# A delta rule with two matrix inversions interleaved half a period apart, and four smaller edits around it

## What is computed

```python
decay = exp(where(incl, g[..., :, None] - g[..., None, :], -inf))
m = where(strict, einsum('bhncd,bhnsd->bhncs', k_beta, k) * decay, 0.0)
t_inv = triangular_solve(eye + m, eye, left_side=True, lower=True, unit_diagonal=True)
...
def step(state, inp):                       # over 16 chunks of 64 tokens
    v_new = u_i - w_i @ state
    o = (q_i * exp(g_i)) @ state + a_i @ v_new
    state = state * exp(g_last) + k_dec.T @ v_new
...
scores = where(|k_pos - q_pos| <= WINDOW, q @ k.T * HD ** -0.5, -inf)
mx = maximum(max(scores), sink);  p = exp(scores - mx)
out = (p / (sum(p) + exp(sink - mx))) @ v
```

## Time and profile before

| what | us |
|---|---|
| median of three runs | 2195.47 |
| the profiled execution | 2197.01 |
| its span, first to last instruction | 2195.2 |
| TensorE (PE) busy | 2104.6, 96% |
| VectorE (DVE) busy | 1120.2, 51% |
| ScalarE (ACT) busy | 725.2, 33% |
| GpSimd (POOL) busy | 353.0, 16% |
| mean granted TensorE clock | 0.980 of full |
| `delta_and_window`, 336 to 716 us of the span | 380 |
| `mix_and_hidden_layer`, about 1332 to 2195 us | 863 |

### The profile page before, as it was taken

How to read it: one execution, slowest core, us unless ns; L and a number is a source line. 1 busy time by engine, 2 the same in 40 slices (tenths; PEclk the granted TensorE clock), 3 DMA queues, 4 the chain that set the end, 5 groups by cost and what they waited for, 6 DMA issues and landing times. The chain is left out here.

```text
span 2195.2 us, 33712 instructions
## 1 busy us (share of the span) xinstructions
PE 2104.6 (96%) x14274; PEld 1637.5 (75%) x14290; DVE 1120.2 (51%) x1724; ACT 725.2 (33%) x1344; POOL 353.0 (16%) x291
## 2 busy tenths in 40 slices
PE   7999997899998899999998999999999999999998
PEld 6888885567676687887775667778888888878877
DVE  6773335766756666563533664464433443442443
ACT  4113313333344334132314773452212212221221
POOL 3000003321322543021210323430000000000000
PEclk9999997999989899999999999999999999999999
DMA  6112322000000847712123103211111111111112
GB/s 217 48 48 86 96 87 92 1 2 2 2 2 2 302 139 275 266 40 58 59 78 150 52 17 135 77 58 48 39 58 48 38 57 51 43 39 53 49 34 101
DMA packets 186890, 167.40 MB, mean 76 GB/s; under 512 B 13472, under 2 KB 163828, under 8 KB 186100
## 3 DMA queue, kind: packets, MB, share of 16 engines
q1 hardware_dynamic: 180974, 146.75, 21.1%
q0 software_dynamic: 4784, 17.83, 2.1%
q10 hardware_dynamic: 982, 0.65, 0.1%
HBM read 138.48 MB, written 26.74 MB: 75 GB/s over the span
## 5 line engine op out<-in xcount | busy, mean ns | idle before, releaser
L250 PE MATMUL mix_acc<-mix_hi,w_hi 128*128 128x512 f32 x1040 | 415.0, 399 | 0.0
L252 PE MATMUL mix_acc<-mix_hi,w_lo 128*128 128x512 f32 x1040 | 409.3, 394 | 0.0
L251 PE MATMUL mix_acc<-m_lo,w_hi 128*128 128x512 f32 x1040 | 408.8, 393 | 0.0
L230 ACT ACTIVATE w_hi<-w_stage 128x1024 fp32r<-128x1024 f32 x154 | 162.6, 1056 | 463.3 <-PE mix_acc L252 247.2
L3178 DVE SCALAR_TENSOR_TENSOR hidden<-mix_acc,hidden_conv,hidden 128x1023 f32<-128x1023 f32 x88 | 112.8, 1282 | 263.5 <-ACT hidden L3127 262.0
L238 DVE TENSOR_TENSOR w_lo<-w_stage,w_hi 128x1024 fp32r<-128x1024 f32 x154 | 192.9, 1252 | 106.3 <-ACT w_hi L230 106.3
L250 PEld LDWEIGHTS mix_acc<-mix_hi,w_hi 128*128 128x128 f32 x1040 | 195.3, 188 | 52.0 <-issue 8.2
L252 PEld LDWEIGHTS mix_acc<-mix_hi,w_lo 128*128 128x128 f32 x1040 | 195.3, 188 | 45.7
L251 PEld LDWEIGHTS mix_acc<-m_lo,w_hi 128*128 128x128 f32 x1040 | 195.5, 188 | 43.4
L250 PE MATMUL acc<-h_hi,w_hi 128*128 128x512 f32 x400 | 156.8, 392 | 0.9 <-issue 0.9
L252 PE MATMUL acc<-h_hi,w_lo 128*128 128x512 f32 x400 | 155.8, 390 | 0.0
(11 more groups left out here) (365 smaller groups left out, 3644.0 us busy)
## 6 DMA issues: line engine op xcount, KB each, us to landing
w_stage<-in_w_in SPq DMA_DIRECT2D x48, 512.0 KB, 3.9
w_stage<-in_w_up SPq DMA_DIRECT2D x44, 512.0 KB, 3.7
w_stage<-in_w_out SPq DMA_DIRECT2D x32, 512.0 KB, 4.1
w_ada<-in_w_ada SPq DMA_DIRECT2D x32, 512.0 KB, 5.1
spill<-y_tok POOLq DMA_DIRECT2D x21, 512.0 KB, 5.1
m_resid<-resid_spill SPq DMA_DIRECT2D x2, 4096.0 KB, 16.9
conv_in<-in_w_ada SPq DMA_DIRECT2D x16, 512.0 KB, 5.6
w_stage<-in_w_down SPq DMA_DIRECT2D x16, 384.0 KB, 3.3
```

What stands on the lines that cost most here:

```text
L230: nc.scalar.activation(w_hi[:, slot], w_stage[:, slot], ACT.Copy).then_inc(w_hi_ready, 1)
L250: nc.tensor.matmul(acc[:, h, :], w_hi[:, slot, k, :], hi[:, k, tok], start=k == 0, stop=False)
L251: nc.tensor.matmul(acc[:, h, :], w_hi[:, slot, k, :], lo[:, k, tok], start=False, stop=False)
L252: mm = nc.tensor.matmul(acc[:, h, :], w_lo[:, slot, k, :], hi[:, k, tok], start=False, stop=k == kts - 1)
```

## The change

It has five parts.

1. Periods are cut into ten slots by the table `CHAIN`. A period s now holds levels 1 and 2 of chunk s and levels 3 to 5 of chunk s - 1, alternately, in two banks `tri[0]` and `tri[1]`; the state's step is that of chunk s - 2. There are 18 periods. `gram` of the next chunk waits only for the inversion two chunks back. `pair_keys` has four buffers and `inv` three.
2. The state's step has one bank, `value_bank`, in place of `kb` and `vb`; `v_rest` and `v_new` have one buffer in place of two; `pairs` writes to `kvb[1]`, and so waits for the state of four chunks before, and `kv_sum` waits for `decay_exp`. POOL scales the values one chunk ahead.
3. `keep_busy` and its 56 matmuls are gone.
4. The mask is added on DVE: `masked` replaces `maxima` with two `tensor_tensor_reduce` in a unit, which read the scores from PSUM and the mask, now float32, from SBUF, and write the negated scores to `prob`; `probs` takes its exponentials in place there. The 64 mask products of `score` are gone, and `score` waits for DVE, no longer for ACT. Window steps sit in slots 1 to 9 only, so a period holds nine and they end in period 16.
5. A placeholder of 128 bytes, `mix2_start`, is placed before the operands of the last stage and no longer behind them; by the same allocation `m_hi` then lies at byte 196352 and `m_lo` at 163584, both multiples of 256.

The diff, cut to its core, with eight spaces of indentation taken off:

```diff
-BF16_GROUPS = ("base16", "late", "swa")
+BF16_GROUPS = ("base16", "late")
...
+PAIR_BUFS, INV_BUFS = 4, 3
+pair_keys = sb("pair_keys", [P, PAIR_BUFS, DN_HEADS, 2, CH], F32, stS)
...
-inv = sb("inv", [P, 2, 2, DN_HEADS, CH], F32, stS)
-v_rest = sb("v_rest", [P, 2, DN_HEADS, DN_DIM], F32, stS)
+inv = sb("inv", [P, INV_BUFS, 2, DN_HEADS, CH], F32, stS)
+v_rest = sb("v_rest", [P, DN_HEADS, DN_DIM], F32, stS)
...
-v_new = sb("v_new", [P, 2, DN_HEADS, DN_DIM], F32, stS)
+v_new = sb("v_new", [P, DN_HEADS, DN_DIM], F32, stS)
...
-tri = bank("tri", where=stS)
-kb = bank("kb", (P, DN_HEADS, DN_DIM), stS)
-vb = bank("vb", (P, DN_HEADS, DN_DIM), stS)
-pair_bank = vb.rearrange("p h (i c) -> p h i c", i=2)
+tri = [bank(f"tri{i}", where=stS) for i in range(2)]
+value_bank = bank("value_bank", (P, DN_HEADS, DN_DIM), stS)
 kvb = [bank(f"kvb{i}", (P, DN_HEADS, DN_DIM), stS) for i in range(2)]
 ob = kvb[0]
+pair_flat = kvb[1].rearrange("p h n -> p (h n)")
+pair_bank = kvb[1].rearrange("p h (i c) -> p h i c", i=2)
...
-GAPS = [(0, 0), (0, 1), (1, 0), (1, 1), (2, 1), (3, 0), (3, 1), (4, 1), (5, 0), (5, 1)]
+CHAIN = (("corner", 1, 3), ("corner", 0, 1), ("inverse", 1, 3), ("inverse", 0, 1), ("corner", 1, 4), ("corner", 0, 2),
+         ("inverse", 1, 4), ("inverse", 0, 2), ("corner", 1, 5), ("inverse", 1, 5))
+SLOTS, PERIODS = len(CHAIN), NCH + 2
+CORNER_AT, MASK_AT, SUM_AT, INV_AT = {}, {(0, 0): 1}, {}, {(0, 0): 2}
...
+def chain_step(s, k):
+    kind, behind, lv = CHAIN[k]
+    n = s - behind
+    return (kind if 0 <= n < NCH else None), n, lv
...
-PREP_FROM, WINDOW_FROM = len(GAPS), 2 * len(GAPS) + 4
...
+PREP_FROM, WINDOW_FROM = SLOTS, 2 * SLOTS + 4
+window_slots = [g for g in range(WINDOW_FROM, PERIODS * SLOTS) if g % SLOTS]
+STEP_AT = dict(zip(window_slots, WINDOW_STEPS))
...
-            if n >= 2:
-                pool.wait_ge(s_vsum, n - 1)
+            if n:
+                pool.wait_ge(s_vsum, n)
...
-        for s in range(NCH + 1):
+        v_scaled(0)
+        decayed(0)
+        for s in range(1, PERIODS):
+            if s == 1:
...
-            if s < NCH:
-                pool.wait_ge(s_xu, STORED * s + 2)
-                v_scaled(s)
-                if s + 1 < NCH:
...
+            n = s - 2
+            if 0 <= n < NCH - 1:
+                v_scaled(n + 1)
+            if 0 <= n < NCH - 2:
+                decayed(n + 1)
+            if n >= 0:
...
-            if n >= 2:
-                pe.wait_ge(s_vnew, n - 1)
-            nc.tensor.matmul(vb.rearrange("p h n -> p (h n)"), identb, late[:, x, :], start=True, stop=False)
+            if n >= 4:
+                pe.wait_ge(s_st, n - 3)
+            nc.tensor.matmul(pair_flat, identb, late[:, x, :], start=True, stop=False)
...
-            if n:
-                pe.wait_ge(s_xu, STORED * n)
+            if n >= 2:
+                pe.wait_ge(s_xu, INV_AT[n - 2, LEVELS - 1])
...
+                    mm = nc.tensor.matmul(value_bank[r, h, :], inv[r, n % INV_BUFS, kind_of(n, hf), h, :],
+                                          v_rest[r, h, :], start=True, stop=True)
...
+            pe.wait_ge(s_pair, min(n + 4, NCH))
...
-        def fill_before_corner(n, lv):
-            if lv == 2 and n in EVEN_STEPS:
-                keep_busy(vb_flat, 3 if n == 2 else 1)
-            if n == NCH - 1 and lv == 2:
-                keep_busy(vb_flat, 3)
-            if n == NCH - 1 and lv in (3, 4):
-                keep_busy(kb_flat, 3)
-        def fill_before_inverse(n, lv):
-            if lv == 1 and (n in EVEN_STEPS or n == NCH - 1):
-                keep_busy(vb_flat, 3)
...
-                pe.wait_ge(s_pr, 2 * u)
+                pe.wait_ge(s_nm, u)
...
                 pe.wait_ge(s_rope, NN)
             for hd in range(2):
-                m0 = (tiles[0] - i + 1) * P
-                nc.tensor.matmul(scb[:, hd, 0:n], identb, swa[:, m0:m0 + n], start=True, stop=False)
-            for hd in range(2):
                 r = rows_of(hd)
                 mm = nc.tensor.matmul(scb[:, hd, 0:n], qk[r, b, i * P:(i + 1) * P],
-                                      qk[r, 4, tiles[0] * P:tiles[0] * P + n], start=False, stop=True)
+                                      qk[r, 4, tiles[0] * P:tiles[0] * P + n], start=True, stop=True)
...
-            if s:
-                state_sums(s - 1)
-            for lv in range(LEVELS):
-                if s < NCH and lv:
-                    fill_before_corner(s, lv)
-                    corner_sum(s, lv)
-                if s and lv == 2:
-                    v_sum(s - 1)
-                if s == NCH and lv == 3:
-                    pe.wait_ge(s_den, 4)
-                    for i in range(TT):
-                        mm = nc.tensor.transpose(scb[0:SW_HEADS, i // 4, i % 4 * P:(i % 4 + 1) * P], rcp[:, i, :],
-                                                 ident)
-                    mm.then_inc(s_mod, 1)
-                if 0 < s < NCH and lv == 4:
-                    kv_sum(s - 1)
-                if s + 1 < NCH and lv == 5:
+        for s in range(PERIODS):
+            z = s - 2
+            for k in range(SLOTS):
+                kind, n, lv = chain_step(s, k)
+                if kind == "corner":
+                    corner_sum(n, lv)
+                elif kind == "inverse":
+                    inv_sum(n, lv)
+                if k == 0 and z >= 0:
+                    state_sums(z)
+                if k == 4 and z >= 0:
+                    v_sum(z)
+                if k == 5 and s + 1 < NCH:
                     pairs(s + 1)
-                if lv:
-                    in_gap(s, lv, 0)
-                if s < NCH and lv:
-                    fill_before_inverse(s, lv)
-                    inv_sum(s, lv)
-                if s and lv == 4:
-                    out_sum(s - 1)
-                if lv == 1 and s in EVEN_STEPS:
-                    keep_busy(vb_flat, 2)
-                in_gap(s, lv, 1)
+                if k == 7 and 0 <= z < NCH - 1:
+                    kv_sum(z)
+                if k == 8 and z >= 0:
+                    out_sum(z)
+                if k == 5 and z == NCH - 1:
+                    turn_reciprocals()
+                in_slot(s, k)
             if s + 1 < NCH:
                 gram(s + 1)
...
-            if n >= 2:
-                act.wait_ge(s_kv, n - 1)
-                act.wait_ge(s_osum, n - 1)
-            nc.scalar.activation(v_new[:, n % 2], vb[:, :, :], ACT.Copy).then_inc(s_vnew, 1)
+            if n:
+                act.wait_ge(s_kv, n)
+                act.wait_ge(s_osum, n)
+            nc.scalar.activation(v_new[:, :, :], value_bank[:, :, :], ACT.Copy).then_inc(s_vnew, 1)
...
             n = len(key_tiles(i)) * P
             act.wait_ge(s_nm, u + 1)
-            if u >= 2:
-                act.wait_ge(s_pt, 2 * u - 2)
             for hd in range(2):
-                nc.scalar.activation(prob[:, u % 2, hd, 0:n], scb[:, hd, 0:n], ACT.Exp,
-                                     bias=max_neg[:, b, i, hd:hd + 1],
+                part = prob[:, u % 2, hd, 0:n]
+                nc.scalar.activation(part, part, ACT.Exp, bias=max_neg[:, b, i, hd:hd + 1], scale=-1.0,
...
-        def maxima(u):
+        def masked(u):
             b, i = att_units[u]
-            n = len(key_tiles(i)) * P
+            tiles = key_tiles(i)
+            n, m0 = len(tiles) * P, (tiles[0] - i + 1) * P
+            if u >= 2:
+                dve.wait_ge(s_pt, 2 * u - 2)
             dve.wait_ge(s_sc, u + 1)
-            nc.vector.reduce_max(row_max[:, u % 2, :], scb[:, :, 0:n], AXX).then_inc(s_rm, 1)
-            dve.wait_ge(s_rm, u + 1)
-            nc.vector.scalar_tensor_tensor(max_neg[:, b, i, :], row_max[:, u % 2, :], -1.0, sink_neg[:, b:b + 5:4],
-                                           ALU.mult, ALU.min).then_inc(s_nm, 1)
+            for hd in range(2):
+                nc.vector.tensor_tensor_reduce(
+                    prob[:, u % 2, hd, 0:n], scb[:, hd, 0:n], swa[:, m0:m0 + n], -1.0,
+                    sink_neg[:, b + 4 * hd:b + 4 * hd + 1], ALU.add, ALU.min,
+                    accum_out=max_neg[:, b, i, hd:hd + 1]).then_inc(s_nm if hd else s_rm, 1)
...
-        for s in range(NCH + 1):
+        first_inverse(0)
+        for s in range(PERIODS):
+            z = s - 2
             if s == 1:
                 small_vectors()
-            if s < NCH:
-                first_inverse(s)
-            in_gap(s, 0, 0)
-            if s:
-                subtract_state(s - 1)
-            for lv in range(LEVELS):
-                if s < NCH and lv:
-                    corner_mask(s, lv)
-                if 0 < s < NCH and lv == 5:
-                    advance(s - 1, 1)
-                if lv:
-                    in_gap(s, lv, 0)
-                if s < NCH and lv:
-                    inv_add(s, lv)
-                if s == 0 and lv == 2:
+            for k in range(SLOTS):
+                kind, n, lv = chain_step(s, k)
+                if kind == "corner":
+                    corner_mask(n, lv)
```

(71 more changed lines are left out.)

171 lines of the change are left out of this document (69 added, 102 removed).

## The result

The kernel after takes 2179.38 us (median of six runs, 2170.92 to 2188.02), the kernel before beside it 2195.18 (2189.65 to 2196.80). The ratio is 0.9928, interval [0.9908, 0.9948]: 16 us faster, where 59 were forecast (2136, range 2110 to 2168). The profiled execution took 2179.81 us, its span is 2178.0.

The account below looks back on a forecast made before the run. PE, busy 96% of the span, was taken to bound the kernel. From 2195.5 us, 44.7 came off for the stage delta_and_window and 15 for the placement of the last stage's operands: 2136 us, range 2110 to 2168.

Parts of the forecast that it names:

- The placement: Last stage: m_hi on a multiple of 256 bytes saves 6.5 ns a matmul; 15 us, between 0 and 17.4.
- The third rival: Last stage: the address doesn't set the pace, DVE and ACT work beside it does; 2151 us, chance 0.10.
- Periods 0, 1, 16 and 17: Ends of delta_and_window: scores_of of chunk 1 at about 348.8 us, then periods of 31.0, 14 and 6.6 us.
- DVE's load: Steady period: stays at 14.8 us, with the mask on DVE costed at nothing.
- The steady period: Periods 3 to 15: 21.7 us less 0.75, 1.0, 0.65 and 0.5 gives 18.8, between 17.9 and 21.3.
- The step that failed: Steady period's waits: those of turns on prob_t copies stay; of 1.9 us of waiting, 0.5 goes in all.
- The bound of 2.0 us: Slower bound on a steady period's waits: each hand-over of slot 9 late by a DVE run, 2.0 us on.
- period 2: In delta_and_window: 28.6 us less fills 2.0, masks 1.2, lower clock 2.7 and a DVE wait 1.6: 21.1.
- The clock: Stage delta_and_window: 5 us added for stretches at the lower clock; a fall for the whole steady stretch had chance 0.05.
- the 2.7 us of period 2: Taken off period 2 for its old 6.8 us at the lower clock.
- the first rival: Granted clock falls to 0.50 for the steady stretch, periods grow to 31.3 us; 2299 us, chance 0.05.
- The second rival: Steady periods: DVE or a hand-over becomes the bound, a period stays at 20.8 us; 2162 us, chance 0.17.

Follow-up runs that it names:

- place_only: The kernel before with part five alone, the placeholder mix2_start placed ahead of the last stage's operands: 2178.95 us, ratio 0.9928.
- place_64: The kernel after with a placeholder of 64 bytes in place of 128, so m_hi and m_lo start 64 past a multiple of 256: 2181.60 us.
- later_moved: The kernel after with probs of the next unit behind copy_turned on ACT, and pairs and decay_exp in the slot of a score from period 3: 2133.93 us.
- probs_later: The kernel after with one ACT item moved: probs of the next unit stands behind copy_turned, in the slot of turn1: 2142.29 us.
- moved_both: The kernel after with masked of slot 9 first on DVE, and pairs and decay_exp in the slot of a turn1 from period 3: 2160.4 us.

## Why the prediction was wrong

- **The placement** was right: 15 us forecast, 16 measured, 178 matmuls in the window. The third rival is out: `place_only` changes the address alone, and `a_hi` keeps its pace beside a slower `mix_hi` in `place_64`.
- **Periods 0, 1, 16 and 17** were right: 349.93 us for 348.8, then 31.1 for 31.0, 13.8 for 14 and 6.5 for 6.6. DVE's load was right too (15.0 us in period 7, 14.8 forecast), so the mask pass cost nothing there.
- **The steady period** was right where nothing queued: nine of the twelve periods 3 to 14 take 19.2 us on average, 18.8 forecast. In `later_moved` all twelve take 18.5 on average.
- **The step that failed** is one sentence on the waits: "The waits of the turns on the copies of `prob_t` stay, since a turn and its copy are still one slot apart." They grew from 5.1 to 27.6 us. The distance in slots was kept, but what stands between on ACT was not looked up: `probs` waits there for DVE's mask pass, `decay_exp` works 1.7 us, and which of them meets the copy depends on the period. `probs_later`, in which nothing but `probs` moves behind the copy, takes 37 us off. The bound of 2.0 us for a hand-over late by a run of DVE was the right size (1.98 in slot 2). But it was laid as a mean on all periods, where the waits come two at a time in every fourth. The copies don't account for period 2, which took 30.2 us for 21.1: the forecast took its old stretch at the lower clock off, and a longer one came (20.5 us) behind waits of 1.6 and 1.4 us that the kernel before has too (3.5 us).
- **The clock** was about half of the miss. It had 5 us in the sum, and 0.05 as a rival that would hold it down for the whole steady stretch. It came in between: 64.9 us low at 0.39 us each are 25 us, 20 above the allowance (16 with the 54.6 us of `place_64`). The price of 0.40 us for each microsecond at 0.50 was right: in the kernel before, the period from 639.36 us on took 28.5 - 21.7 = 6.8 us longer with 17.1 us at 0.50, which is 0.40, and period 7 with and without fills gives 0.39. From it come the 2.7 us of period 2 in the sum and the 18.8 / 0.60 of the first rival. The argument against ("PE's needed work becomes denser") was true of the mean, but not of the microseconds around a late copy. In periods 7 and 11 the clock fell at 504.4, 514.7, 589.8 and 603.4 us, each time within or at most 1.5 us behind a wait of 2.0 to 2.5 us.
- **The account.** The stage ended 43.6 us late: 29.9 in periods 3, 7 and 11, 9.1 in period 2, 3.2 in the other nine, 5.2 from period 15 on and 1.2 before period 2, less the 5 allowed for the clock. With ACT's order mended it ends at 670.4 (670.9 forecast) and the kernel takes 2133.9 (2136). That the end points meet so well is luck in part: period 2 still takes 28.7 us there, for 21.1, and a shorter period 1 (27.5 for 31.0), twelve periods 3 us shorter in all and the 5 us allowed for the clock make up for it. What isn't luck is the steady stretch: PE no longer waits between a level and DVE, as forecast, and with the copies on time too its periods are as short as forecast. The order on ACT that this needs was not in the change.
- The second rival had the right family (a hand-over becomes the bound; it named `prob_t` copies) and too small a size: it laid 20.8 us on all periods, for 2162. The twelve periods came to 21.6 on average, 19.2 in nine and 28.8 in three, and period 2 came on top.

## What to carry to other kernels

When steps are laid on a grid of slots, list for each engine what stands ahead of the item that another engine waits for, in every phase in which the two patterns can meet (here four), and not only how many slots lie between. An item that nobody needs soon, and that waits itself, belongs behind the one that is needed at once. Fills whose only use is to keep the clock up may go once PE's waits have gone, not earlier: leaving them out cost 22 us in the kernel before, while in periods 3 to 14 of `later_moved` the clock stood at 1.00 without any, and eleven put into its period 2 gained nothing in time.

## What the hardware showed

- A wait of PE of about 2 us mostly cost more than itself here: a stretch of 3.4 to 20.5 us at a granted clock of 0.50 followed or began in it, at 0.39 us for each. Of the seven waits of 1.9 us or more at `turn1` in the kernel after, six were followed so, the one at 676 us was not; in `place_64`, whose stage is the same, all seven were. The two waits of period 2, 1.6 and 1.4 us, had 20.5 us at the lower clock behind them in after and none up to the next wait of 1.5 us or more in `place_64` and `moved_both`. Waits of 0.9 to 1.5 us had it in `moved_both` in places (6.8 us low at one of 1.53 that ends at 417.3 us, 3.4 us behind one of 1.12 at 439.4) and not in others (0.91 at 448.7, 1.53 at 585.2), so no border can be read from these runs.
- TensorE's pace on 512 float32 columns depended on where the moving operand starts: 227.0 ns at multiples of 256 bytes, 229.5 at 64 past, 233.5 at 128 past. At 64 past only the products with `mix_hi` are slower (232 and 229 ns), at 128 past those with `m_lo` too (233 to 234 ns on average for each of the three products). Why that is so wasn't tried, nor any other distance.
